# Per-token norms ahead of two feed-forward blocks: the sum spread over all partitions first, the power -1/2 taken on 256 columns

## The reference

```python
def rms_norm_2(x, g):
    xf = x.astype(jnp.float32)
    y = xf * lax.rsqrt(jnp.mean(xf * xf, axis=-1, keepdims=True) + EPS)
    return (y * g.astype(jnp.float32)).astype(x.dtype)

def conv_ffn(h, w_up, conv_w, conv_b, w_down):
    z = h @ w_up
    u = z[..., :D_FF]
    g = dwconv3_centred(z[..., D_FF:], conv_w) + conv_b
    return (jax.nn.gelu(g, approximate=False) * u) @ w_down

    # in each of the two layers
    h = h + conv_ffn(rms_norm_2(h, ffn_norm_g[layer]), ffn_w_up[layer], ...)
```

## Time and profile before

| what | value |
|---|---|
| median of 3 runs | 990.91 us (990.75 to 991.11) |
| span of the profiled execution | 989.2 us |
| median less span | 1.7 us |
| TensorE busy | 972.1 us, 98% |
| VectorE busy | 686.6 us, 69% |
| ScalarE busy | 556.1 us, 56% |
| GpSimd busy | 209.3 us, 21% |
| mean granted TensorE clock | 0.998 |

### The profile page before, as it was taken

One profiled execution on the slowest core, in us unless ns is written; L12 is line 12 of the kernel. 1 busy time (PEld: TensorE's weight loads), 2 busy tenths in 40 slices (PEclk: granted clock), 3 DMA queues, 4 the chain that ended last, 5 costly groups with the idle time before them and its releaser, 6 DMA issues.

```text
span 989.2 us, 16695 instructions
## 1 busy us (share of the span) xinstructions
PE 972.1 (98%) x6532; PEld 879.3 (89%) x6532; DVE 686.6 (69%) x1056; ACT 556.1 (56%) x856; POOL 209.3 (21%) x199
## 2 busy tenths in 40 slices
PE   9999989999999999999999999999999999999997
PEld 8779759989988988798899899999898989989985
DVE  5789785854666687665556779776687665767973
ACT  5556673665765474555355466555445555546662
POOL 0002034300344440012003005221044301202610
PEclk9999999999999999999999999999999999999999
DMA  9634425465334447246414655457546432555441
GB/s 363 241 132 166 175 87 208 162 221 214 128 128 141 174 133 271 108 171 213 150 64 170 213 186 187 181 194 281 186 170 255 163 135 93 198 183 181 172 152 43
DMA packets 24831, 172.93 MB, mean 175 GB/s; under 512 B 2752, under 2 KB 2880, under 8 KB 4416
## 3 DMA queue, kind: packets, MB, share of 16 engines
q1 hardware_dynamic: 23040, 160.66, 45.6%
q10 hardware_dynamic: 1728, 11.40, 3.0%
HBM read 166.81 MB, written 5.24 MB: 174 GB/s over the span
## 4 chain that ended last, share of the span: by engine, by line
PE 93%; DVE 2%; ACT 2%; DMA 1%; issue 1%; POOL 0%; SPq 0%; ACTq 0%; DVEq 0%
PE banks L506 38%; PE banks L594 16%; PE banks L512 14%; PE banks L514 7%; PE banks L504 6%; PE banks L656 4%; PE banks L710 1%; DMA raw<-w 1%; PE banks L761 1%; PE banks L762 1%; DVE work L1725 1%; PE banks L743 1%; PE banks L917 1%; PE banks L834 0%; DVE work L1737 0%
## 5 line engine op out<-in xcount | busy, mean ns | idle before, releaser
L1598 DVE TENSOR_TENSOR wl<-raw,wh 128x1024 fp32r<-128x1024 f32 x300 | 379.7, 1275 | 157.4 <-ACT wh L1090 156.0
L1090 ACT ACTIVATE wh<-raw 128x1024 fp32r<-128x1024 f32 x300 | 313.2, 1054 | 180.6 <-PE banks L506 76.1
L512 PE MATMUL banks<-xx,wh 128*128 128x512 f32 x544 | 192.5, 398 | 0.0
L506 PE MATMUL banks<-xx,wh 128*128 128x256 f32 x1024 | 190.3, 284 | 0.0
L506 PE MATMUL banks<-yy,wh 128*128 128x256 f32 x1024 | 187.8, 285 | 0.1
L506 PEld LDWEIGHTS banks<-xx,wh 128*128 128x128 f32 x1024 | 161.4, 192 | 1.4 <-issue 0.5
L506 PEld LDWEIGHTS banks<-yy,wh 128*128 128x128 f32 x1024 | 160.4, 192 | 0.7 <-issue 0.5
L514 PE MATMUL banks<-xx,wl 128*128 128x256 f32 x544 | 151.8, 279 | 0.0
L506 PE MATMUL banks<-xx,wl 128*128 128x256 f32 x512 | 144.8, 283 | 0.0
L506 PE MATMUL banks<-yy,wl 128*128 128x256 f32 x512 | 138.6, 283 | 0.0
L512 PEld LDWEIGHTS banks<-xx,wh 128*128 128x128 f32 x544 | 102.0, 187 | 22.7
(11 more groups left out here) (221 smaller groups left out, 1449.3 us busy)
## 6 DMA issues: line engine op xcount, KB each, us to landing
raw<-w SPq DMA_DIRECT2D x149, 1024.0 KB, 4.8
m_scratch<-yy ACTq DMA_DIRECT2D x2, 1024.0 KB, 5.9
k_scratch<-kt ACTq DMA_DIRECT2D x2, 1024.0 KB, 8.2
kt<-k_scratch ACTq DMA_DIRECT2D x2, 1024.0 KB, 5.8
yy<-m_scratch ACTq DMA_DIRECT2D x2, 1024.0 KB, 6.0
raw<-w SPq DMA_DIRECT2D x2, 512.0 KB, 5.2
h<-xt SPq DMA_DIRECT2D x2, 512.0 KB, 6.1
v<-memt ACTq DMA_DIRECT2D x1, 1024.0 KB, 7.7
```

The source lines that it names most:

```text
L506: return pe.matmul(b[:, j, :], weights, o_[:, kk, :], start=k0 + k == 0 and q == 0 and (j == 0 or not both_open), stop=k0 + k == KT * p.de ...
L512: pe.matmul(b[:, j, :], wh[:, slot, j, k * P:k * P + P], operand[:, :, tile0 + k0 + k, :], start=k0 + k == 0, stop=False, skip_group_check ...
L1090: act.activation(wh[:, n % 2, j, :], raw[:, n % RAW_SLOTS, j, :], ACT.Copy).then_inc(hi_ready, 1)
L1598: dve.tensor_tensor(wl[:, n % 2, j, :], raw[:, n % RAW_SLOTS, j, :], wh[:, n % 2, j, :].bitcast(F32), ALU.subtract).then_inc(lo_ready, 1)
```

## The change

For "ffn0" and "ffn1" alone, stats and bcast are replaced by one matmul of ones by acc, at the place of stats. It leaves each token's sum on all partitions of bank 5, 256 columns. VectorE scales these into rb (128x256), GpSimd raises rb to the power -1/2 in place, and VectorE waits for that before it empties the first chunk. The two diagonals, the broadcast matmul and ScalarE's copy fall away for these two norms. The counts of the semaphores that the other norms use are made anew without them.

```diff
+SPREAD = ('ffn0', 'ffn1')
+DIAG = bases(*[(u, 1) for u in POW if u not in SPREAD])
+RBS = bases(*[(u, 1) for u in ("mem", "mix0", "xa0", "ffn0", "mix1", "xa1", "ffn1") if u not in SPREAD])
@@ TensorE
+            def spread_sums(name):
+
+                pe.wait_ge(acc_done, ACC[name] + 4)
+                pe.matmul(bank[5][:, 0:S], ones[:, :], acc[:, :], start=True, stop=True).then_inc(st_full, 1)
...
             def norm_hooks(name):
+                if name in SPREAD:
+                    return {(1, 0, 1): lambda: spread_sums(name)}
                 return {(1, 0, 1): lambda: stats(name), (1, 1, 0): lambda: bcast(name)}
@@ ScalarE
             def spreading(name):
 
+                if name in SPREAD:
+                    return None
+
@@ VectorE
             def inverse_rms(name, eps):
 
                 dve.wait_ge(st_full, POW[name] + 1)
+                if name in SPREAD:
+                    dve.tensor_scalar(rb[:, :], bank[5][:, 0:S], 1.0 / D, eps, ALU.mult, ALU.add).then_inc(st_read, 1)
+                    return
...
             def times_rb(dst, name=None, low=None):
 
                 def f(c, b):
-                    if c == 0 and name is not None:
+                    if c == 0 and name in SPREAD:
+                        dve.wait_ge(st_pow, POW[name] + 1)
+                    elif c == 0 and name is not None:
                         dve.wait_ge(rb_ready, RBS[name] + 1)
@@ GpSimd
             def power(name):
                 pool.wait_ge(st_read, POW[name] + 1)
+                if name in SPREAD:
+                    pool.tensor_tensor(rb[:, :], rb[:, :], half[:, 0:1].broadcast_to([P, S]), ALU.pow).then_inc(st_pow, 1)
+                    return
```

More of the change, by code:

```diff
@@ L194 @@
 POW = bases(*[(u, 1) for u in ("mem", "var0", "var1", "mix0", "xa0", "ffn0", "mix1", "xa1", "ffn1")])
-RBS = bases(*[(u, 1) for u in ("mem", "mix0", "xa0", "ffn0", "mix1", "xa1", "ffn1")])
+SPREAD = ('ffn0', 'ffn1')
+DIAG = bases(*[(u, 1) for u in POW if u not in SPREAD])
+RBS = bases(*[(u, 1) for u in ("mem", "mix0", "xa0", "ffn0", "mix1", "xa1", "ffn1") if u not in SPREAD])
 SQ = bases(*[(u, 4) for u in POW])
@@ L676, in sums @@
                 pe.matmul(bank[5][:, 0:S], ones[:, :], acc[:, :], start=True, stop=True).then_inc(mean_full, 1)
+            def spread_sums(name):
+                pe.wait_ge(acc_done, ACC[name] + 4)
+                pe.matmul(bank[5][:, 0:S], ones[:, :], acc[:, :], start=True, stop=True).then_inc(st_full, 1)
             def bcast(name):
-                pe.wait_ge(st_diag, 2 * POW[name] + 2)
+                pe.wait_ge(st_diag, 2 * DIAG[name] + 2)
                 pe.matmul(bank[5][:, 0:S], ones[:, :], diag[:, :, :].rearrange("p a b -> p (a b)"),
@@ L1175, in spread @@
             def spread(name, dst=rb):
-                act.wait_ge(bc_full, POW[name] + 1)
+                act.wait_ge(bc_full, DIAG[name] + 1)
                 act.activation(dst[:, :], bank[5][:, 0:S], ACT.Copy).then_inc(rb_ready, 1)
@@ L1856, in layer_norm @@
                     if c == 2:
-                        dve.wait_ge(bc_full, POW["var" + l] + 1)
+                        dve.wait_ge(bc_full, DIAG["var" + l] + 1)
                         for m in range(KT):
```

## The result

The changed kernel takes 1074.16 us (1073.57 to 1074.94), against 990.91: a ratio of 1.084, interval 1.0827 to 1.0852.

What follows compares the result with a forecast made beforehand. TensorE, busy 98% of the span, was taken to bound the kernel. Per block, 26.65 us later at the third chunk, saving included, plus 2.2 for the clock; twice that, 57.7, on 990.9 gave 1048 us, range 1000 to 1075.

Steps and rivals of the forecast that it cites:

- The power: GpSimd's 256-column power, from the split's end at 853.7 to 882.4, at 111 ns a column; TensorE's third chunk waits.
- I take 111, because it is the difference of two clean durations: GpSimd's power: each further column costs 111 ns, from 700 ns for two columns less 589 for one.
- The second reading: GpSimd's power, read from the long one-column row: a clean column is 0.56 us and the step 140 ns.
- The clock: TensorE behind its wait at the third chunk runs at half speed at first: 2.2 us a block, between 0 and 5.6.
- The wait for the split: GpSimd's power, ready at 852.6, gets its data only when VectorE's weight split ends at 853.7.
- TensorE's pieces: Second fu1 chunk: sums and broadcast (0.60 and 0.43 us) become one matmul at 0.43, saving 0.60 us per norm.
- Rival A: GpSimd's power costs about an add, ending at 854.3; TensorE doesn't wait at the third chunk: 989.7 us, chance 15%.
- The rule that I set beside it: GpSimd two-input operations stream at about 2.6 cycles an element: some 0.6 us for 256 columns, but stated of adds.
- Rival B: GpSimd's power gets cheaper by the column on long rows: 1017.5 us at 50 ns a column, chance 19%.
- C: GpSimd's power has no fixed part, 350 ns a column; TensorE restarts 87.4 us late: 1170 us, chance 4%.

Runs made afterwards that it cites:

- experiment eight: Changed kernel, but GpSimd raises 16, 1, 2, 3, 4 and 8 columns one after another in each block, other columns left without the power: 1008.92 us.
- experiment four: Changed kernel plus 88 matmuls of 256 columns into an unused bank between second and third chunk of each fu block: 1070.57 us.
- experiment two: Changed kernel with the power only on the first 16 columns in the first block and the first 128 in the second: 1013.92 us.
- experiment one: Changed kernel with GpSimd multiplying the 256 columns by -1/2 instead of raising them to it: 991.27 us beside 991.13 of the kernel before.

## Why the prediction was right, and where its size was off

The direction, the place and the mechanism are as told. TensorE waits at the third chunk of each fu block, nowhere else; VectorE stands at the new wait with the emptying behind it; nothing is won back. 1074.2 lies within the range of 1000 to 1075, at its very upper end, and 26 us above the 1048 that I named. That it lies inside is in part luck: the range's top was 1070, from 140 ns a column and 5.6 us for the clock, rounded up. The column cost more than that top allows and the clock less, and the one covered the other.

- The power. It was forecast at 28.7 us from the end of the split on; measured 580.62 - 539.63 = 41.0. That is 12.3 us a block and 24.6 of the 26 us. The step that was mis-sized is "I take 111, because it is the difference of two clean durations": the 589 ns were not clean (experiment eight; L2083 lay beside them), and 255 columns made 37 ns into 9.4 us. The second reading, 0.56 us for a clean column and 140 ns a step, was nearer: 0.552 and 150. It used the same row through what lay beside it. The remaining 9 ns a column are those by which later columns cost more than the first steps, 0.159 against 0.150.
- The clock. Taken as 2.2 us a block from the program's start; measured 2.2 and 1.9, and 3.6 for both by experiment four. The agreement is luck: the granted clock is 1.00 in the first 7 us of the trace, so the start was no case of a lower clock, and the prediction says itself that its rows show none.
- The wait for the split. The power was to be ready at 0.1 us behind the split's start and held until its end; it was, with 0.89 us by the line of experiment two (0.95 by my 853.7 - 852.6 less the 0.15 ahead of the data).
- TensorE's pieces. Forecast 0.60 us a block less; 0.49 measured in the chunk (experiment one), 0.41 without the change of pace, and not measurable in the time, with two or with five. The new matmul was charged at the broadcast's 0.43; in experiment one it takes some 0.7 out of the product (two pairs and the matmul 1.40 us, from 850.47 to 851.87, two pairs alone 0.70). The old sums took 0.72 by the same count (850.95 to 852.37), not 0.60.
- Rival A fell by experiments one and two: the same form costs an add's price with a multiplication, and 0.159 us a column with the power. The rule that I set beside it, about 2.6 cycles an element for two inputs (the Trainium skill, GPSIMD Engine Reference, section 3.1, Elementwise), gives an estimate of some 0.6 us; it holds here for the multiplication, which ended 0.47 us behind the split and so took 0.62 with the 0.15 ahead of the data, and not for the power. Rival B fell by the straight line from 16 to 256 columns, C by the clean single column.

## What to carry to other kernels

A price by the element, read from the difference of two tiny instructions, is multiplied by the length: look for a second reading of the same rows, see what every engine did beside each of them before calling one clean, and where the two differ leave room beyond both. Here both readings, 111 and 140 ns, lay below the 159 measured. Spreading a small tensor over all partitions before a costly function saves a TensorE piece and makes the function longer by every column of the row; here 0.49 us were bought with 41. An engine that is 27% busy can still set the time, when another engine's queue stands still for it.

## What the hardware showed beyond that

- GpSimd's power costs 0.38 us and 0.159 us a column of 128 partitions, in a straight line from 1 to 256 columns but for the first few (0.150).
- VectorE's reciprocal of 128x256 fp32 takes 1.75 us, where a scaling of the same size takes 0.42.
- A VectorE product of two SBUF tiles beside a 42 us power on GpSimd took 0.84 us, where one with a bank as its second input took 0.41; it did not wait for the power's end.
- After 39 us of standing still, TensorE ran at the granted clock 0.50 for 4.6 us (582.27 to about 586.9) and lost 2.2 us by it; in the second block it lost 1.9.
- The same loop of matmuls ran at 5.55 or at 5.65 us a chunk in different kernels, and at 0.347 or 0.354 us a pair within one chunk of the kernel before, the granted clock at 1.00 throughout.
